# Launch of a two-layer decoder kernel: x and the first weights laid out by the host, first block's transfers on two queues, second block in its own banks

## The reference

```python
def sandwich(x, pre, post, fn, weight):
    return x + weight * rms_norm(fn(rms_norm(x, pre)), post)

def swiglu(h, wg, wu, wd):          # wg, wu: 1024 x 2816, wd: 2816 x 1024
    return (jax.nn.silu(h @ wg) * (h @ wu)) @ wd
...
x = sandwich(x, ffn1[0], ffn1[1], functools.partial(swiglu, wg=ffn1[2], wu=ffn1[3], wd=ffn1[4]), MACARON_WEIGHT)
```

## Time and profile before

| | |
|---|---|
| time, median of 3 runs | 970.74 us (970.66 to 970.95) |
| time of the profiled execution | 970.93 us, of which the span of the profile is 969.1 us |
| TensorE busy in the span | 960.2 us (99%) |
| VectorE, ScalarE, GpSimd busy | 777.5, 501.0, 128.1 us |
| first product of the first block starts | 6.15 us |
| first block's gate and up, second block's, `down(0)`: their last products start | 20.05, 31.86, 37.30 us |

### The profile page before, as it was taken

One profiled execution on the slowest core, in us unless ns is written; L12 is line 12 of the kernel. 1 busy time (PEld: TensorE's weight loads), 2 busy tenths in 40 slices (PEclk: granted clock), 3 DMA queues, 4 the chain that ended last, 5 costly groups with the idle time before them and its releaser, 6 DMA issues.

```text
span 969.1 us, 13599 instructions
## 1 busy us (share of the span) xinstructions
PE 960.2 (99%) x4701; PEld 811.6 (84%) x4701; DVE 777.5 (80%) x1511; ACT 501.0 (52%) x813; POOL 128.1 (13%) x144
## 2 busy tenths in 40 slices
PE   8999999999999999999999999999999999999997
PEld 6888888899888888888888888888889888888886
DVE  6788988758669888888898878878779588888884
ACT  7434353678563534344645353466668465353432
POOL 5000000055610000000200000013242520000000
PEclk9999999999999999999999999999999999999999
DMA  9784747242674666567175747626750435656531
GB/s 308 248 279 157 257 163 260 82 143 88 189 237 161 201 212 215 175 207 237 55 271 167 256 147 243 217 88 199 263 179 18 152 109 201 233 193 197 200 104 43
DMA packets 126734, 178.12 MB, mean 184 GB/s; under 512 B 3258, under 2 KB 103700, under 8 KB 126688
## 3 DMA queue, kind: packets, MB, share of 16 engines
q1 hardware_dynamic: 122784, 170.63, 52.7%
q10 hardware_dynamic: 3088, 5.51, 1.8%
q0 software_dynamic: 816, 1.37, 0.5%
HBM read 176.41 MB, written 1.09 MB: 183 GB/s over the span
## 4 chain that ended last, share of the span: by engine, by line
PE 97%; DVE 1%; DMA 1%; ACT 0%; SPq 0%; issue 0%; DVEq 0%; POOLq 0%; POOL 0%; ACTq 0%
PE ps L1219 93%; PE ps L1473 1%; PE ps L1257 1%; DMA raw<-in_l_ffn_wu 1%; PE ps L1233 0%; PE ps L1611 0%; DVE w_lo L1749 0%; SPq L543 0%; DVE end_hi L2062 0%; PE ps L1330 0%; DVE down_lo L2053 0%; SPq L520 0%; DVE w_lo L1763 0%; ACT w_hi L846 0%; ACT logit L1016 0%
## 5 line engine op out<-in xcount | busy, mean ns | idle before, releaser
L1219 PE MATMUL ps<-w_hi,xt_hi 128*128 128x512 f32 (+3 forms) x912 | 354.0, 388 | 0.9 <-ACT w_hi L846 0.5
L1219 PE MATMUL ps<-w_lo,xt_hi 128*128 128x512 f32 (+3 forms) x912 | 351.3, 385 | 0.1
L1219 PE MATMUL ps<-w_hi,xt_lo 128*128 128x512 f32 (+3 forms) x912 | 351.3, 385 | 0.0
L1749 DVE TENSOR_TENSOR w_lo<-raw,w_hi 128x2048 fp32r<-128x2048 f32 (+3 forms) x107 | 234.6, 2232 | 49.8 <-ACT w_hi L830 49.4
L1841 DVE STREAM_TRANSPOSE ps<-h 32x128 f32<-32x128 f32 x624 | 201.4, 323 | 9.2
L830 ACT ACTIVATE w_hi<-raw 128x2048 fp32r<-128x2048 f32 (+3 forms) x110 | 200.0, 1865 | 6.8 <-DMA raw<-in_l_ffn_wu 4.1
L1219 PEld LDWEIGHTS ps<-w_hi,xt_hi 128*128 128x128 f32 x912 | 171.3, 188 | 33.9 <-DVE xt_lo L1778 0.8
L1219 PEld LDWEIGHTS ps<-w_lo,xt_hi 128*128 128x128 f32 x912 | 171.3, 188 | 33.6 <-DVE w_lo L1763 1.2
L1219 PEld LDWEIGHTS ps<-w_hi,xt_lo 128*128 128x128 f32 x912 | 171.2, 188 | 33.3
L934 ACT ACTIVATE ht_hi<-ps 128x512 fp32r<-128x512 f32 x40 | 24.0, 599 | 290.8 <-DVE ps L1841 286.8
L1219 PE MATMUL ps<-down_hi,ht_hi 128*128 128x512 f32 x320 | 124.9, 390 | 0.0
(11 more groups left out here) (235 smaller groups left out, 868.4 us busy)
## 6 DMA issues: line engine op xcount, KB each, us to landing
raw<-in_l_ffn_wg SPq DMA_DIRECT2D x42, 1024.0 KB, 7.3
raw<-in_l_ffn_wu SPq DMA_DIRECT2D x42, 1024.0 KB, 9.8
raw_down<-in_l_ffn_wd SPq DMA_DIRECT2D x40, 1024.0 KB, 5.0
raw<-in_l_w_in SPq DMA_DIRECT2D x5, 2048.0 KB, 7.9
raw<-in_l_w_out SPq DMA_DIRECT2D x4, 2048.0 KB, 7.8
xn<-in_l_ffn_wd SPq DMA_DIRECT2D x4, 1024.0 KB, 7.2
raw<-in_l_w_in SPq DMA_DIRECT2D x2, 1536.0 KB, 7.5
gpost<-in_l_ffn_post ACTq DMA_DIRECT2D x4, 512.0 KB, 5.8
```

Source lines behind the costliest of these rows:

```text
L1219: return pe.matmul(dst, lhs, rhs, start=start, stop=stop, skip_group_check=True)
L1749: dve.tensor_tensor(part(w_lo), part(raw), part(w_hi).bitcast(F32), ALU.subtract).then_inc(main_lo, 1)
```

## The change

The host lays out what the launch needs: one array `first` with, for each partition, the 8 gains of the first norm and then for each of 8 chunks 256 columns of x already turned and the 512 gate and up columns of the first block; one array `first_main` with the second and third block in the order of the buffers; one array `small` (128 x 539) with the gains, small matrices, rotary tables and sinks as columns; and the bias rows ready but for their sign. The transfers of the first block (6 pieces of 1, 1, 1, 1, 2, 2 chunks) go by turns on SyncE's and ScalarE's queue, the second block's (the same sizes) on SyncE's. The third block's are two of 8 KB per partition. x itself still comes, for the mean squares and the residual.

TensorE no longer turns x, the gains or the table at the launch. It takes the first block chunk by chunk with both tiles, and the second block too, with the turning of the first h in its middle; the second block's gate and up go to banks 7 (tile 0) and 3 (tile 1). Bank 3 is also the last of the four banks of down, so one wait is new there. The first two chunks' `xt_hi` are made by VectorE, the others by ScalarE.

```diff
-    FIRST_PIECES = ((1, 1, 2, 2, 2), (2, 2, 2, 2))
-    WITH_MAIN = ((3, 4), (1, 3))
+    FIRST_PIECES = ((1, 1, 1, 1, 2, 2), (1, 1, 1, 1, 2, 2))
+    WITH_MAIN = ((4, 5), (3, 5))
...
+        def gu_bank(u, jc, t):
+            return (7, 3)[t] if u == 0 and isinstance(jc, int) and jc == 1 else 4 + t
...
+        def first_main(queue, i):
+            k, size = first_start(0, i), FIRST_PIECES[0][i]
+            cols = slice(0 if i == 0 else KD + k * (SEQ + 512), KD + (k + size) * (SEQ + 512))
+            queue.dma_start(first[:, cols], a["first"][:, cols]).then_inc(first_landed[0][i], 16)
...
+            def first_blocks():
+
+                for i in range(0, len(FIRST_PIECES[0]), 2):
+                    first_main(sp, i)
+                load_x(0)
+                second_main(0)
+                second_main(1)
+                load_x(1)
+                for i in range(2, len(FIRST_PIECES[1])):
+                    second_main(i)
...
-            act.dma_start(grows0, a[f"{STAGES[0]}_pre"].rearrange("(c p) -> c p", p=P)).then_inc(gains_landed, 16)
-            load_x(act, 0, parts=(1,))
...
+            for i in range(1, len(FIRST_PIECES[0]), 2):
+                first_main(act, i)
             load_table(ACT.Silu)
...
+                for i in range(len(FIRST_PIECES[0])):
+                    act.wait_ge(first_landed[0][i], 16)
+                    for k in range(max(first_start(0, i), BY_DVE), first_start(0, i) + FIRST_PIECES[0][i]):
+                        act.activation(xt_hi[:, k, :], first_xt[:, k, :], ACT.Copy, scale=first_gain[:, k:k + 1])\
+                           .then_inc(first_x_hi, 1)
+                    split_first(0, i)
+                act.wait_ge(x_landed[0], 16)
                 x_squares(0, 0)
                 split_first(1, 0)
+                split_first(1, 1)
+                act.wait_ge(x_landed[1], 16)
+                x_squares(0, 1)
...
+            def first_terms(n, chunks, tiles=range(TILES)):
+
+                for k in chunks:
+                    piece = [i for i in range(len(FIRST_PIECES[n])) if first_start(n, i) == k]
+                    for i in piece:
+                        with_main, count = first_count(n, i)
+                        pe.wait_ge((first_hi, main_hi)[with_main], count)
+                    if n == 0:
+                        x_is_high(pe, k)
+                    for t in tiles:
+                        mm(ps[:, gu_bank(0, n, t), :], xt_hi[:, k, t * P:(t + 1) * P], main_view(w_hi, n, k, 512), k == 0, False)
+                    if n == 0:
+                        pe.wait_ge(first_x_lo, k + 1)
...
                     for part in range(2):
                         pe.wait_ge(d_lo, g(2 * (d0 + jc) + part + 1, 2))
                         for t in tiles:
+                            if u == 0 and isinstance(jc, int) and jc == 0 and (t, part) == (1, 1):
+                                pe.wait_ge(h_ready, 2 * 2)
                             ins = rows_product(jc, t, part, usual)
...
-                    turn_x(s_no, 0, between={2: lambda: keep_busy(6)})
-                    for t, lo, hi in ((0, 0, 2), (1, 0, 2), (0, 2, 4), (1, 2, 4), (0, 4, 8), (1, 4, 8)):
-                        if (t, lo) == (1, 0):
-                            turn_x(s_no, 1)
-                        ins = product(0, t, 512, 4 + t, chunks="norm0", span=range(lo, hi))
-                        if hi == KD:
-                            ins.then_inc(gu_ready, 1)
+                def first_blocks():
+
+                    first_terms(0, range(0, 8))
+                    first_terms(1, range(0, 4))
+                    turn_first()
+                    first_terms(1, range(4, 8))
...
-            keep_busy(8)
-            pe.wait_ge(gains_landed, 16)
-            pe.transpose(ps[:, 3, 0:8], grows0, ident[0:8, 0:8]).then_inc(prep_ready, 1)
...
+            keep_busy(17)
+            ffn(0, 0)
```

More of the change, by code:

```diff
@@ L55 @@
 CROW = 32
+G_Q, G_KV, G_PEK, G_PEV, G_COLS = 48, 50, 51, 67, 83
+S_W2V = G_COLS
+S_W2K = S_W2V + 2 * HEAD
+S_ROPE = S_W2K + 4 * HEAD
+S_SINKS = S_ROPE + TILES * ROPE
+S_COLS = S_SINKS + HEADS
+ROW = SEQ + P
 FB = 256
@@ L78, in bucket_ranges @@
                      * np.float32(BUCKETS - exact)).astype(np.int32)
[L79 to L84, removed]
+    return np.where(n < exact, n, np.minimum(large, BUCKETS - 1))
 def trunk(nc, a, out):
@@ L180, in trunk @@
         ps = ctx.enter_context(nc.psum_tensor("ps", [P, 8, 512], F32))
+        with nc.sbuf_tensor("lead", [P, 2 * HEADS * SEQ + MAIN], F32) as lead:
+            pass
+        bias = sb("bias", [P, 2 * HEADS, SEQ])
         raw = sb("raw", [P, 2, MAIN])
@@ L217, in trunk @@
         cmp_ok = sb("cmp_ok", [P, TILES, CPAD])
[L218 to L221, removed]
+        small = sb("small", [P, S_COLS])
         half = sb("half", [P, 1])
@@ L513, in t_bank_two, with x_is_high @@
             return ps[:, t_banks[job], :].rearrange("p (k t) -> p k t", k=2)
[L516 to L520, removed]
+        BY_DVE = 2
+        def x_is_high(eng, k):
+            eng.wait_ge(*((first_x_dve, k + 1) if k < BY_DVE else (first_x_hi, k + 1 - BY_DVE)))
         def load_bias(queue, first, count, landed):
@@ L534, in ffn_main @@
                 dst = raw[:, n % 2, :].rearrange("p (k two c) -> p k two c", two=2, c=FB)
[L537 to L546, removed]
+                for i, part in enumerate(("wg", "wu")):
+                    src = a[f"{w}_{part}"].rearrange("(k p) n -> p k n", p=P)[:, :, cols]
+                    sp.dma_start(dst[:, :, i, :], src).then_inc(main_landed[n % 2], 16)
             def ffn_down(w, j):
@@ L1306, in product, with ffn, gate_up @@
                 return ins
-            def ffn(u, s_no, aside=None):
+            def first_terms(n, chunks, tiles=range(TILES)):
[10 more added lines that the diff above has]
+                        pe.wait_ge(first_x_lo, k + 1)
+                    for t in tiles:
+                        mm(ps[:, gu_bank(0, n, t), :], xt_lo[:, k, t * P:(t + 1) * P], main_view(w_hi, n, k, 512), False, False)
+                    for i in piece:
+                        with_main, count = first_count(n, i)
+                        pe.wait_ge((first_lo, main_lo)[with_main], count)
+                    for t in tiles:
+                        ins = mm(ps[:, gu_bank(0, n, t), :], xt_hi[:, k, t * P:(t + 1) * P], main_view(w_lo, n, k, 512), False,
+                                 k == KD - 1)
+                        if k == KD - 1:
+                            ins.then_inc(gu_ready, 1)
+            def ffn(u, s_no):
                 n0, d0 = first_block[STAGES[s_no]], u * FBLOCKS
-                def gate_up(jc, g, between=None, tiles=range(TILES)):
+                def gate_up(jc, g, tiles=range(TILES)):
                     n = n0 + jc
@@ L1314, in gate_up @@
                     for t in tiles:
-                        if t == 1 and between:
-                            between()
                         if d0 + jc >= 1:
@@ L1881, in first_step @@
                     mul(0, 0, fixed)
-                    for i in range(1, 4):
-                        split_first(1, i)
+                    split_first(1, 2)
                     mul(0, 1, fixed)
+                    split_first(1, 3)
+                    split_first(1, 4)
+                    split_first(1, 5)
                 if u == 0:
@@ L2289 @@
     arrays, args = {}, {}
-    given = {name: np.ascontiguousarray(inputs[name]) for name in _INS}
-    given["rope_tables"] = rope_tables()
+    given = {name: inputs[name] for name in _INS}
+    given.update(laid_out(inputs))
     for name, value in given.items():
+        value = np.ascontiguousarray(value)
         arrays[f"in_{name}"] = value
```

212 lines of the change are left out of this document (95 added, 117 removed).

## The result

The changed kernel takes 974.69 us (median of 6 runs, 973.54 to 976.63) against 970.72 us (970.64 to 971.12): ratio 1.0041, 95% interval 1.0031 to 1.0052. It is 4.0 us slower; forecast were 971.2 us and at most 973.4.

What follows compares the result with a forecast made beforehand. TensorE, busy 960.2 of 969.1 us, was taken as the bound. Start and turnings (-2.7) plus the new wait (+3.2) gave +0.5, and 971.2 us when added to the median 970.74; range 969.4 to 973.4.

Steps and rivals of the forecast that it cites:

- First part: when is the first block done?: Launch: first block ends at 18.05, second at 29.4 against 32.09 before, so 2.7 us won.
- E: The second block's end on TensorE, forecast at 29.4 us.
- its share: Launch transfers: ScalarE's queue takes about 1.3 MB while SyncE's three pieces, 1.58 MB, flow.
- A rule weighed: New wait in `down(0)`: 3.2 us is too short to lower TensorE's clock, despite the skill's warning; the sum stays.
- The second rival: The clock falls in the new wait or the launch's pauses, losing 2 us: 973.2; chance 0.07.
- Second part: the new wait: In `down(0)` TensorE waits 3.2 us for `mul(1, 1)`; third block starts at E + 8.6, not E + 5.44.
- Break-even: Second block's end at 28.9, with chunks 4 and 5 landed at 9.9.
- The third block's transfer: Ahead of the third block's split: lands at 28, hidden by 1.8 us before the split starts at 29.8.
- Edits at nothing: VectorE's bias rows, GpSimd's 15 transfers and later small inputs: no TensorE row waits for them, so no effect.
- a launch dense from 5.1 us on: Launch upper limit: everything dense from when data can be there, about 5.1, wins 4.7 us.

Runs made afterwards that it cites:

- second profile: The changed kernel run again with no edit, against the kernel before: 974.92 us, ratio 1.0042; the span of its profile is 972.7.
- one-queue kernel: The changed kernel with all six pieces of the first block on SyncE's queue, in order: 972.91 us, ratio 1.0018 against the kernel before.
- the version with both edits: The changed kernel with `silu(1, 1)` and `mul(1, 1)` ahead of the third block's split and all first-block pieces on SyncE's queue: 967.90 us, ratio 0.9969.

## Why the prediction was wrong

The sum of the forecast was -2.7 + 3.2 = +0.5 us. Measured at the third block's first product, in the profile in which the clock held, it was -1.1 + 3.3 = +2.2; the clock adds 1.4 in the second profile and, by the other runs, 1.5 to 1.7 in the median.

1. **"First part: when is the first block done?" failed**, where it has chunks 0 to 3 end at 10.6 to 11 and chunks 4 and 5 on SyncE's queue decide. The landing of these two was forecast for 10.4 and came near 9.8, which by the forecast's own working is E = 28.8. But the sum has no term for the landing of chunks 1 and 3 on ScalarE's queue. Chunk 1 landed at about 8.0 and TensorE waited for it; chunk 3 landed at 10.84, and its splits stand ahead of those of chunks 4 and 5 on ScalarE. With that the forecast's own chain gives the end: 10.84 + 0.93 (chunk 3's `xt_hi` and `w_hi`) + 7.65 = 19.42; the second block started at 19.62. I gave ScalarE's queue "its share" of the bytes from the start; it got none until 4.8 us, and from 6 us on, with smaller packets, less than half. Price 1.6 us of E, and the one-queue kernel gave 1.7 back.
2. **"A rule weighed" failed.** I took the clock as kept, since at the end of the span it fell about 4 us after the last product. It fell around the new wait in nine of ten runs of this kernel, by their mean granted clock, and the warning that the forecast weighed and set aside is what these runs bear out. The second rival had it at a chance of 0.07 and a price of 2 us; the price was about right and the chance was not. A row of a fall behind a longer idle time is no evidence that a shorter one is safe.
3. **"Second part: the new wait" was right**, in its place, its cause and its size: 3.3 us lost against 3.2 (2.99 of them idle), E + 8.75 against E + 8.6. Break-even by that working was E = 28.9; E was 30.95.
4. **The third block's transfer** was hidden, as forecast: the split starts at E + 0.37 right behind silu, and the transfer, issued at 17.27, landed 10.6 us later at 27.9 (forecast 28).
5. **"Edits at nothing"** held in the launch. In the profiled run 0.5 us more is lost at 710 us, in the second layer's attention, where TensorE waits for VectorE's copy `probt`. That copy stands behind a split, which stands behind ScalarE's, which waits for a weight transfer:

```profile
703.13 3.72 ACT L853 ACTIVATE w_hi<-raw 128x2048 fp32r<-128x2048 f32 x2 [2.48 <-DMA raw<-in_l_w_in]
```

Before, the same wait of ScalarE is 0.33 us (at 698.87). The packed `small` plays no part in it. The profile of the same kernel again shows no such wait of TensorE, and the version with both edits 0.2 us.
6. Of the 4.0 us, 2.2 are launch and new wait and 1.4 to 1.7 the clock. The 0.1 to 0.4 left are within what the runs of the kernel before differ by, and I can't place them. One sum is off without effect: a launch dense from 5.1 us on would have won 4.9 us, not 4.7.

Why ScalarE's queue moves nothing for its first three microseconds wasn't tried by itself and stays open; that putting all on one queue takes the loss away is shown.

## What to carry to other kernels

A spare buffer only moves a wait unless the work that frees it comes earlier too: look at what stands ahead of the releasing instruction on its own engine. Here two instructions moved past a split were worth 4.5 us, more than the 3.1 us that the launch won even with one queue (the second block ends at 29.01 there, at 32.09 before). Pieces that are wanted in order came in order on one queue and out of order on two, so each piece's landing needs a term of its own where two queues share a stream. And a pause of some microseconds on TensorE is priced with what the clock may take behind it.

## What the hardware showed that I had not expected

A second queue's transfer, issued at 1.57 us, moved its first bytes at about 4.8, when the first queue had moved about what it was given up to 1.57, and with packets of 3 KB against 6 KB it then got 0.13 MB in a microsecond (7:8) against 0.28. By the mean granted clock, a pause of 3.0 us in `down(0)` lowered the clock in 9 of 10 runs of one kernel and 8 of 10 of another; the three profiles that show it have 1.2 GHz for 3.4, 3.4 and 6.8 us. A pause of 3.1 us in the launch left it up, as did one of 2.0 us in at least 7 of 9 runs. What decides between them is open.

The clock column reads 1.00 in the whole launch, and yet in the second profile of after TensorE's first products are about as far apart as behind the pause (two rows of two products each start 0.86 us apart), before the wait for chunk 1:

```profile
6.23 1.04 PE L1242 MATMUL ps<-w_hi,xt_lo 128*128 128x512 f32 x2
7.09 0.66 PE L1242 MATMUL ps<-w_lo,xt_hi 128*128 128x512 f32 x2
```

So for the first microseconds the distance of the products says more than the column. It cost nothing here, as chunk 1 was not there before 8.
